# Layer 1's input projection computed as two by two block products with seven half products for eight

## The reference

```
z = h @ w_in        # h: 512 tokens x 1024, w_in: 1024 x (r,k,v,lora | q,k,v | q,k,v,o,gates | merge gates)
```

## Time and profile before

| | us |
|---|---|
| median of the runs | 2697.51 |
| the profiled execution | 2697.61 |
| its span, first to last instruction | 2695.8 |
| PE busy in the span | 2354.9 |
| DVE busy | 1177.3 |
| ACT busy | 727.6 |
| layer 1's projection, from its first matmul (1560.49) to the next stage's first instruction (1788.20) | 227.7 |

### The profile page before, as it was taken

The page is one execution under the profiler, slowest core; times in us unless marked ns, Lnnn a source line. Parts: engine busy times, 40 slices in busy tenths (PEclk is TensorE's granted clock), DMA queues, the critical chain, the costliest instruction groups (busy, mean ns, idle before and its releaser), DMA issues. The chain is left out here.

```text
span 2695.8 us, 49410 instructions
## 1 busy us (share of the span) xinstructions
PE 2354.9 (87%) x20164; PEld 1525.7 (57%) x20164; DVE 1177.3 (44%) x2620; ACT 727.6 (27%) x1706; POOL 381.6 (14%) x402
## 2 busy tenths in 40 slices
PE   6999989879979997998989589999879988797785
PEld 3444455459944444465655455557658877654443
DVE  3877764578842114532212610024668842521113
ACT  2101165444431003122222110034534430221120
POOL 0000000213430001132221000000213320222210
PEclk9999999989989997999999899999989989798998
DMA  8555301200024102699996822222200033699895
GB/s 367 199 245 211 125 32 49 79 34 4 5 103 194 71 0 83 254 405 375 362 357 237 343 102 94 94 71 90 99 31 4 4 123 126 258 403 384 339 348 221
DMA packets 78258, 466.69 MB, mean 173 GB/s; under 512 B 17104, under 2 KB 29008, under 8 KB 49616
## 3 DMA queue, kind: packets, MB, share of 16 engines
q1 hardware_dynamic: 53584, 413.14, 39.1%
q0 software_dynamic: 24448, 50.38, 4.9%
HBM read 440.12 MB, written 61.08 MB: 186 GB/s over the span
## 5 line engine op out<-in xcount | busy, mean ns | idle before, releaser
L523 PE MATMUL win_ps<-h,win_ring 128*128 128x512 f32 (+1 forms) x1024 | 397.9, 550 | 10.1 <-PEq L293 5.4
L2445 PE MATMUL xp_psG<-moe_ring,rt_xt 128*64 128x256 f32 (+1 forms) x2048 | 329.6, 407 | 19.0 <-DMA moe_ring<-in_moe 18.7
L523 PEld LDWEIGHTS win_ps<-h,win_ring 128*128 128x128 f32 x1024 | 196.3, 193 | 202.6 <-issue 195.6
L2445 PEld LDWEIGHTS xp_psG<-moe_ring,rt_xt 128*64 128x64 f32 (+1 forms) x2048 | 227.8, 164 | 98.3 <-issue 42.1
L583 DVE SCALAR_TENSOR_TENSOR mod_acc<-ada_ring,cv_silu,mod_acc 128x512 f32<-128x512 f32 x280 | 198.0, 748 | 10.8 <-issue 0.4
L2466 PE MATMUL xp_psY<-moe_ring,rt_aT 128*64 128x512 f32 (+1 forms) x512 | 162.2, 603 | 10.5 <-DVE rt_aT L2718 10.5
L2326 POOL DMA_INDIRECT y_rows<-rt_y,rt_dst x84 | 84.3, 1003 | 488.9 <-DVE rt_y L2723 268.7
L2711 DVE TENSOR_TENSOR rt_sg<-rt_sg,xp_psG 128x128 f32<-128x128 f32 x84 | 24.2, 288 | 287.5 <-ACT rt_sg L2517 287.5
L1813 PE MATMUL sc_ps<-sc_NT,sc_XI 64*64 64x64 f32 x2560 | 145.2, 219 | 0.1
L2430 PE MATMUL xp_psT<-cst,rt_xg 128*128 128x128 f32 x672 | 93.9, 285 | 55.4 <-DMA rt_xg<-h_rows,rt_tok 55.2
L2430 PEld LDWEIGHTS xp_psT<-cst,rt_xg 128*128 128x128 f32 x672 | 76.9, 144 | 114.3 <-DMA rt_xg<-h_rows,rt_tok 83.8
(11 more groups left out here) (459 smaller groups left out, 3984.1 us busy)
## 6 DMA issues: line engine op xcount, KB each, us to landing
moe_ring<-in_moe SPq DMA_DIRECT2D x128, 1536.0 KB, 13.1
ada_ring<-in_ada SPq DMA_DIRECT2D x22, 2048.0 KB, 15.2
win_ring<-in_win SPq DMA_DIRECT2D x20, 2048.0 KB, 8.0
cb_yg<-y_rows SPq DMA_DIRECT2D x16, 1024.0 KB, 12.2
mg_ring<-in_mg SPq DMA_DIRECT2D x16, 768.0 KB, 4.4
mg_wo<-in_wo SPq DMA_DIRECT2D x2, 4096.0 KB, 13.7
pr<-y_rows SPq DMA_DIRECT2D x8, 1024.0 KB, 18.6
ml_gate_ring<-in_mg SPq DMA_DIRECT2D x12, 512.0 KB, 3.7
```

The costliest lines, as they stand in the source:

```text
L523: last = pe.matmul(ps[:, n % NB, first(n):T], ring[:, j % 2, c, m * P:(m + 1) * P], h[:, c, first(n):T], start=c == 0, stop=c == KD - 1)
L2445: last = pe.matmul(psG[at:at + m, u % 2, 0:2 * P].rearrange("p (q n) -> p q n", q=2), xt[:, u % 2, c, at:at + m], ring[:, slot, c:2 * KD:K ...
```

## The change

Layer 1's projection is done by a new function; layer 0 keeps the old one. Two neighbouring full tiles make a pair: a product of a 2 by 2 block matrix (two tiles by two halves of the 1024 channels) with a 2 by 2 block matrix (two halves of the channels by two halves of 256 columns). A pair has seven products of 128x256 over 4 chunks each, on sums of blocks, and DVE adds the seven results together. There are 12 pairs, in blocks 1, 2, 3, 5, 6, 8 and 9. The 15 half tiles and one full tile (the second half of block 3's last two) are computed as before, and called singles here: there are 28 units.

- The operands' sums. `right_sums` makes four arrays of 128 x 1024 out of `h`, once. `left_sums` makes four arrays of 128 x 512 out of the weights of a pair, eight times, into two buffers in turn, and twice out of `h` for blocks 8 and 9. For these two blocks the right sums are made of the weights. Each is four DVE operations with two drains. All other sums than the first are asked for behind a pair's last addition, at a place given by `ready(i)`, which is not before the unit that frees the weights' ring slot.
- The order of products is p1, p2, p6, p7, p4, p5, p3. The first two need no sums. PE waits for the sums at the third.
- PSUM is a ring of eight banks. A product's matmuls wait for the copy or the addition that read the bank eight products ago.
- ACT copies p1 and the singles; DVE makes seven operations of 128x256 a pair, of which six release a bank.
- SP loads block j when the last unit of block j-2 is done.

```
+PRODUCTS = ("p1", "p2", "p6", "p7", "p4", "p5", "p3")
+def left_sums(dve, out, a):
+    dve.tensor_tensor(out[:, 0], a(1, 0), a(1, 1), ALU.add)
+    dve.tensor_tensor(out[:, 2], a(0, 0), a(1, 0), ALU.subtract)
+    dve.drain()
+    dve.tensor_tensor(out[:, 1], out[:, 0], a(0, 0), ALU.subtract)
+    dve.drain()
+    return dve.tensor_tensor(out[:, 3], a(0, 1), out[:, 1], ALU.subtract)
...
+def stage_projection_by_seven(nc, k, l, h, pr, pn, vna, vml):
+    NBLK, NB = 10, 8
...
+            @block.sync
+                sp.dma_start(k.d_h, h[:]).then_inc(h_saved.sem, 16)
+                for j in range(2, NBLK):
+                    sp.wait_ge(done.sem, done.at(block_end[j - 2]))
+                    load_projection(sp, k, l, j)
...
+            @block.tensor
+                def free(q):
+                    if q >= NB:
+                        pe.wait_ge(act_out.sem, act_out.at(copied[q - NB]))
+                        pe.wait_ge(dve_out.sem, dve_out.at(added[q - NB]))
...
+                    for f, name in enumerate(PRODUCTS):
+                        q = first_of[u] + f
+                        free(q)
+                        if f == 2:
+                            if j < 8:
+                                pe.wait_ge(lefts.sem, lefts.at(pair_of[u] + 1))
+                                pe.wait_ge(rights.sem, rights.at(1))
...
+                        x, y = operands_of(name, a, lefts_of, b, rights_of)
+                        for c in range(HK):
+                            last = pe.matmul(ps[:, q % NB, 0:256], x[:, c], y[:, c], start=c == 0, stop=c == HK - 1)
+                        last.then_inc(done.sem, 1)
...
+            @block.vector
+                def weight_sums(i):
+                    dve.wait_ge(win_in[j % 2].sem, win_in[j % 2].at(j // 2 * 16 + 16))
+                    if i >= 2:
+                        dve.wait_ge(done.sem, done.at(first_of[by_weights[i - 2]] + 7))
+                    left_sums(dve, left[:, i % 2], w_tile(j, m)).then_inc(lefts.sem, 1)
+                def ready(i):
+                    j = units[by_weights[i]][1]
+                    return max(i - 2, *(x for x in range(i) if units[by_weights[x]][1] <= max(j - 2, 1)))
...
+                right_sums(dve, right, h_part).then_inc(rights.sem, 1)
+                for n in (*range(R_T, R_T + KC), GD_T):
+                    dve.memset(pr[:, n, 0:CTX], 0.0)
+                weight_sums(0)
+                weight_sums(1)
+                for i in range(2):
+                    left_sums(dve, token[:, i], h_tile(2 * i)).then_inc(tokens.sem, 1)
+                for u, (pair, j, m) in enumerate(units):
...
+                    dve.tensor_tensor(home(j, n, 0), shaped(product("p2"), n), shaped(one, n), ALU.add)
+                    dve.tensor_tensor(own[:, 0], product("p6"), one, ALU.add)
+                    dve.drain()
+                    dve.memset(k.scratch[:, 0:1], 0.0).then_inc(taken.sem, 1)
+                    dve.tensor_tensor(own[:, 1], product("p7"), own[:, 0], ALU.add)
+                    dve.drain()
+                    dve.tensor_tensor(home(j, n + 1, 0), shaped(own[:, 1], n), shaped(product("p4"), n), ALU.subtract)
+                    p5 = product("p5")
+                    dve.tensor_tensor(own[:, 2], p5, own[:, 0], ALU.add)
+                    dve.tensor_tensor(home(j, n + 1, 1), shaped(p5, n), shaped(own[:, 1], n), ALU.add)
+                    dve.drain()
+                    dve.tensor_tensor(home(j, n, 1), shaped(product("p3"), n), shaped(own[:, 2], n), ALU.add)
+                    for i in range(2, len(by_weights)):
+                        if p == ready(i):
+                            weight_sums(i)
+                    if p == len(by_weights) - 1:
+                        feature_sums(8)
+                    if u == len(units) - 4:
+                        feature_sums(9)
...
-                        stage_projection(nc, k, l, h, pr, pn, vna, vml)
+                        (stage_projection_by_seven if l else stage_projection)(nc, k, l, h, pr, pn, vna, vml)
```

More of the change, by code:

```diff
@@ L609, in stage_projection, with right_sums @@
             s.advance(16 * len(range(j, NA, 3)))
+PRODUCTS = ("p1", "p2", "p6", "p7", "p4", "p5", "p3")
[6 more added lines that the diff above has]
+    return dve.tensor_tensor(out[:, 3], a(0, 1), out[:, 1], ALU.subtract)
+def right_sums(dve, out, b):
+    dve.tensor_tensor(out[:, 0], b(0, 1), b(0, 0), ALU.subtract)
+    dve.tensor_tensor(out[:, 2], b(1, 1), b(0, 1), ALU.subtract)
+    dve.drain()
+    dve.tensor_tensor(out[:, 1], b(1, 1), out[:, 0], ALU.subtract)
+    dve.drain()
+    return dve.tensor_tensor(out[:, 3], out[:, 1], b(1, 0), ALU.subtract)
@@ new lines, in operands_of, with first, sb, h_part @@
+def operands_of(name, a, left, b, right):
+    return {"p1": (lambda: (a(0, 0), b(0, 0))), "p2": (lambda: (a(0, 1), b(1, 0))), "p3": (lambda: (left[:, 3], b(1, 1))),
+            "p4": (lambda: (a(1, 1), right[:, 3])), "p5": (lambda: (left[:, 0], right[:, 0])),
+            "p6": (lambda: (left[:, 1], right[:, 1])), "p7": (lambda: (left[:, 2], right[:, 2]))}[name]()
+def stage_projection_by_seven(nc, k, l, h, pr, pn, vna, vml):
+    NBLK, NB = 10, 8
+    HK = KD // 2
+    (done, act_out, dve_out, taken, lefts, tokens, rights, h_saved) = k.signals(
+        "win_product", "win_copied", "win_added", "win_pair", "win_left", "win_token_left", "win_right", "h_saved")
+    win_in, ring = k.win_in, k.win_ring
+    late = {R_T + c for c in range(KC)} | {GD_T} | {16 + t for t in (*range(NQ_T, NQ_T + 4), MQ_T, MQ_T + 1, *range(MO_T, MO_T + 4))}
+    def first(n):
+        return CTX if n in late else 0
+    units = []
+    for j in range(NBLK):
+        for m in (0, 2):
+            n = 4 * j + m
+            if n in late and n + 1 in late or n == GD_T:
+                units += [(False, j, m), (False, j, m + 1)]
+            else:
+                units.append((True, j, m))
+    NP = sum(u[0] for u in units)
+    first_of, pair_of, ends, bank = [], [], [], 0
+    for pair, j, m in units:
+        first_of.append(bank)
+        pair_of.append(sum(u[0] for u in units[:len(first_of) - 1]))
+        bank += 7 if pair else 1
+    copied, added = [], []
+    for pair, j, m in units:
+        for name in PRODUCTS if pair else ("one",):
+            by_act = name in ("one", "p1")
+            copied.append(by_act + (copied[-1] if copied else 0))
+            added.append((not by_act) + (added[-1] if added else 0))
+    with ExitStack() as ctx:
+        def sb(name, shape):
+            return ctx.enter_context(nc.sbuf_tensor(f"win_{name}{l}", shape, F32))
+        ps = ctx.enter_context(nc.psum_tensor(f"win_ps{l}", [P, NB, 512], F32))
+        right = sb("right", [P, 4, HK, 256])
+        left = sb("left", [P, 2, 4, HK, P])
+        token = sb("token", [P, 2, 4, HK, P])
+        p1 = sb("p1", [P, 2, 256])
+        tmp = sb("tmp", [P, 2, 3, 256])
+        right9 = left[:].rearrange("p s f c n -> p (s f c n)").rearrange("p (f c n) -> p f c n", f=4, c=HK)
+        def h_part(i, q):
+            return h[:, i * HK:(i + 1) * HK, q * 256:(q + 1) * 256]
+        def w_tile(j, m):
+            return lambda i, q: ring[:, j % 2, q * HK:(q + 1) * HK, (m + i) * P:(m + i + 1) * P]
+        def h_tile(m):
+            return lambda i, q: h[:, q * HK:(q + 1) * HK, (m + i) * P:(m + i + 1) * P]
+        def w_part(j):
+            return lambda i, q: ring[:, j % 2, i * HK:(i + 1) * HK, q * 256:(q + 1) * 256]
+        def sides(u):
+            pair, j, m = units[u]
+            if j < 8:
+                return w_tile(j, m), left[:, pair_of[u] % 2], h_part, right
+            return h_tile(m), token[:, m // 2], w_part(j), right if j == 8 else right9
+        def home(j, n, q):
+            if n < 32:
+                return (pr if n < 16 else pn)[:, n % 16, q * 256:(q + 1) * 256]
+            if n < 36:
+                return vna[:, n % 4, q * 256:(q + 1) * 256]
+            return vml[:, n % 4, 2 * q:2 * q + 2, 0:P]
+        def shaped(x, n):
+            return x.rearrange("p (h v) -> p h v", v=P) if n >= 36 else x
+        by_weights = [u for u, x in enumerate(units) if x[0] and x[1] < 8]
+        block_end = {units[u][1]: first_of[u] + (7 if units[u][0] else 1) for u in range(len(units))}
+        with nc.Block(no_gpsimd_drain=True) as block:
+            @block.sync
+            def _(sp):
+                sp.dma_start(k.d_h, h[:]).then_inc(h_saved.sem, 16)
+                for j in range(2, NBLK):
+                    sp.wait_ge(done.sem, done.at(block_end[j - 2]))
+                    load_projection(sp, k, l, j)
+                sp.wait_ge(h_saved.sem, h_saved.at(16))
+            @block.tensor
+            def _(pe):
+                def free(q):
[3 more added lines that the diff above has]
+                for u, (pair, j, m) in enumerate(units):
+                    pe.wait_ge(win_in[j % 2].sem, win_in[j % 2].at(j // 2 * 16 + 16))
+                    if not pair:
+                        n = 4 * j + m
```

(78 more changed lines are left out.)

## The result

Six runs of the changed kernel gave a median of 2672.5 us (2670.45 to 2677.77), against 2692.65 (2687.12 to 2698.64) for six of the kernel before: ratio 0.9922, 95% interval 0.9904 to 0.994, 20.2 us less. The forecast was 19.6 us less, from 2697.6 to 2678.0.

The account below looks back on a forecast made before the run. The prediction took PE alone to bound layer 1's projection; -19.8 for matmuls, +0.4 for a late call and -0.2 at the end made -19.6 us, from 2697.61 to 2678.0 us, range 2670 to 2688.

Parts of the forecast that it names:

- Matmuls: Layer 1's projection: a pair falls from 13.733 to 12.085 us, so 12 pairs save 19.8 us.
- Boundaries: 60 more places in the pairs where PE passes waits: bounds 0 to 3.6 us, taken as 0.
- Rival A: In the pairs, boundaries cost 3.6 us (first half) and late sums 1.5 us more: 2683 us; chance 0.11.
- rival B: Each product in the pairs loses 0.235 us, about one exposed weight load: 2697 us, no change; chance 0.08.
- DVE's additions and sums: In the pairs, 79 us of new DVE busy time, hidden behind PE; bounds 0 to 1.2 us, taken as 0.
- The opening: Stage's beginning: DVE's first sums and memsets run from 1560.6 to about 1578.5, hidden, with 11 us to spare.
- The late call: Block 2's first pair: sums asked for directly ahead of use stall PE once by 0.2 to 0.5 us, taken +0.4.
- Sums behind a load: Blocks 5 and 8: sums that wait for a block's load stay hidden, with 6.5 and 4.3 us to spare.
- Banks: PSUM in the stage: eight banks give 12 us of slack against a DVE lag of at most 6; no bound.
- The end: Stage's last work: an addition of 0.42 us replaces a copy of 0.60 us, -0.2 us.
- Rival C: Brief PE stops in the pairs lower the clock to 1.2 GHz for part of the stage: 2727 us; chance 0.05.
- signs of being wrong: PE waiting for DVE every pair, products over 1.75 us, clock under 0.97, or later stages giving back over 3 us.

Follow-up runs that it names:

- asked early: The changed kernel with ready(i) = i - 2, so weight sums are asked for as soon as their buffer is free: 2689.54 us, ratio to the kernel before 0.9982.

## Why the prediction was right

- *What bounds it.* PE alone, and the next stage only moves: the stage's 19.8 us are the program's 20.2 within its interval (1 - 0.994 to 1 - 0.9904 of 2692.65 is 16.2 to 25.8 us). That interval is wide, and that 20.2 lies 0.6 from the forecast is in part luck; the stage's 19.84 (19.68 without its first tile) is the measurement that bears the sum out.
- *Matmuls, -19.8.* Pairs at 12.085 us, 12 of them; the eighth product put back gives +20.5. The shape kept its pace, as the half tiles' rows said.
- *Boundaries, 0 of 0 to 3.6.* The forecast's argument that a tile's pace is exactly 8 or 16 times the matmul's went in a circle, as the matmul's pace was got by dividing the tile's (and 16 x 0.4316 is 6.91, not 6.867). It was true all the same: in the traces before and after, once the clock is at 1.00, MATMUL records start 0.429 us apart at 128x512 and 0.216 at 128x256, across boundaries as inside tiles, except at the first two records of pair 2's third product (0.372 and 0.290). Rival A's first half and rival B fall: a run of pairs shows 3.453 us for two products, and twelve eighth products with no new boundary restore the old time to 0.8 us (221.76 against 220.95), which is the 0.08 us by which eight narrow products (13.81) are longer than two tiles (13.73), twelve times, less the 0.18 of the end. The end taken, that of the stage's own rows, was the right one; the attention's 0.06 did not carry over.
- *DVE's additions and sums, hidden.* 0.42 us an addition and 2.7 a set of weight sums, as its rows show, 75 us in all where 79 were forecast, most of the difference (3.2 us) being operations that overlap where there is no drain. Doubling the weight sums shows how hidden.
- *The opening.* Forecast to end at 1578.5; the last token sum ends at 1577.01 + 0.69 = 1577.7.
- *The late call, +0.4.* Place and mechanism right, size 0.23, inside 0.2 to 0.5. Shown by moving the call. The forecast that the waits would list it was wrong: gaps this short are seen only in the spacing of starts.
- *Sums behind a load.* 4.3 us to spare were forecast for block 8. Its sums end at 1718.27 and the third product starts at 1722.49: 4.2. Against block 5, 6.5 were forecast: its first sums end at 1659.16 and are wanted at 1665.51, 6.4.
- *Banks.* Not a bound; it takes a cut to two to see any of it.
- *The end, -0.2.* The last work is DVE's 0.42 us at 1767.58 in place of ACT's 0.60: 0.18.
- *Rival C.* The clock stayed at 1.00 through all pairs: PE went through eight banks, and in one run through two, without a fall of the clock. The Trainium skill (TensorE: Matmul & The Clock Gate, section "A second HAM failure mode: psum-queue depth-cycling") tells of a kernel whose clock falls and rises as PE idles briefly between groups while it cycles through PSUM banks; the traces here don't show that. What they show is the price of one long stop ("asked early", 11.2 us and 0.50). That many brief stops would bring the clock down is shown by no run here.
- *The range.* It took the spread of whole times from three runs, 7 us. Nineteen runs of the kernel before later spanned 2683.63 to 2701.66, 18 us, so a median of three could have strayed further than the range allowed for. The measured 2672.5 lies 2.5 us above the low end of 2670, brought there by the kernel before's median and not by a term of the sum. The last of the forecast's signs of being wrong, 3 us in the stages behind, is finer than one pair of traces can show, as those stages spread by 6.1.

## What to carry to other kernels

Where PE bounds a stage and matmuls of the halved shape still hide their weight loads, seven products for eight give nearly an eighth of the paired matmul time back (19.8 of 164.8 us here); read the halved shape's pace from a row of the same stage first. What decides is the other engine's order of work, not its load: a call placed ahead of a load that waits for PE's own progress cost 14 us, while making all weight sums twice cost 3. Read the stage's length between two fixed events; it repeated to 0.01 us in two traces here where whole times spread by 18.

## What the runs showed of the hardware

A stop of TensorE of 11.2 us within a stage brought the granted clock to 0.50, and the work behind it ran at that level for some 5.5 us, 2.8 us lost on top of the stop; a stop of 3.2 us left it at 1.00. With weight loads busy 53.08 of 60.60 us, matmuls of 128x256 in groups of four, each group behind up to four satisfied waits, kept their pace of 0.4316 us across all boundaries but one; what a late operand cost there, 0.23 us, did not show in PE's busy time (60.60 of 60.60) but in the starts.
